# Passes ordered by the weight's part, and 512-column passes in the memory heads' pairs too

## The reference, cut to what matters

```python
h = rms_norm(x, g_pre)                                # x: 512 tokens x 2048
proj = einsum('bsd,de->bse', h, w_in)                 # fp32, all heads' q, k, v and gates
out_a = moba_attention(...)                           # 6 heads, block-sparse causal
out_b = forgetting_attention(...)                     # 6 heads, with a cumulated forget gate
out_m = memory_attention(qm, km, vm)                  # 4 heads into 256 memory tokens
y = concat([out_a * silu(ga), out_b * silu(gb), out_m * silu(gm)])
x = x + rms_norm(einsum('bse,ed->bsd', y, w_out), g_post)
```

## Time and profile before

| | |
|---|---|
| median of 3 runs | 901.62 us (901.34 to 902.13) |
| the profiled execution | 902.28 us, span 900.5 us |
| granted TensorE clock | 0.993 |
| PE busy | 871.3 us, 97% of the span |
| PEld busy | 764.1 us, 85% |
| DVE busy | 733.1 us, 81% |
| ACT busy | 537.8 us, 60% |
| POOL busy | 76.6 us, 9% |
| a weight piece of 512 KB (`raw<-in_w_in`), from issue to landing | 5.4 us, median of 112 |

### The profile page before, as it was taken

The page is one execution under the profiler, slowest core; times in us unless marked ns, Lnnn a source line. Parts: engine busy times, 40 slices in busy tenths (PEclk is TensorE's granted clock), DMA queues, the critical chain, the costliest instruction groups (busy, mean ns, idle before and its releaser), DMA issues.

```text
span 900.5 us, 13815 instructions
## 1 busy us (share of the span) xinstructions
PE 871.3 (97%) x5181; PEld 764.1 (85%) x5181; DVE 733.1 (81%) x1070; ACT 537.8 (60%) x932; POOL 76.6 (9%) x84
## 2 busy tenths in 40 slices
PE   8998999999999999999999999999999999999995
PEld 6888998987888888888888888888888877778884
DVE  5889978888888888888888888888988885975558
ACT  5794665555656565656565656565656585565452
POOL 0000220000000000000030303030301000000000
PEclk9999999999999999999999999999999999999998
DMA  9961567467668568667667667567653397465854
GB/s 304 284 167 48 164 165 154 118 174 164 165 142 210 151 167 185 154 175 177 152 176 175 153 175 175 152 176 175 152 129 106 130 364 272 154 220 189 290 199 186
DMA packets 179143, 161.37 MB, mean 179 GB/s; under 512 B 7353, under 2 KB 144217, under 8 KB 177670
## 3 DMA queue, kind: packets, MB, share of 16 engines
q1 hardware_dynamic: 169942, 141.62, 51.2%
q0 software_dynamic: 8704, 16.78, 13.6%
q10 hardware_dynamic: 432, 2.10, 0.7%
HBM read 152.33 MB, written 43.28 MB: 217 GB/s over the span
## 4 chain that ended last, share of the span: by engine, by line
PE 71%; DVE 15%; ACT 8%; issue 5%; POOL 1%; DVEq 0%; ACTq 0%; POOLq 0%
PE d_ps L703 18%; PE e_ps L703 10%; PE d_ps L705 9%; PE e_ps L705 5%; PE c_ps L703 4%; DVE ring L1459 3%; PE pt_ps L810 3%; ACT ring L1017 3%; PE c_ps L705 2%; PE d_ps L653 2%; PE d_ps L655 2%; PE d_ps L654 2%; DVE sums L1486 2%; PE score_ps L654 1%; PE score_ps L655 1%
## 5 line engine op out<-in xcount | busy, mean ns | idle before, releaser
L1459 DVE TENSOR_TENSOR ring<-raw,ring 128x1024 fp32r<-128x1024 f32 x134 | 164.7, 1231 | 53.1 <-ACT ring L1017 53.0
L703 PE MATMUL d_ps<-late,ring 128*128 128x512 f32 x576 | 206.6, 398 | 1.2 <-DVE five L1586 1.2
L1459 DVE TENSOR_TENSOR ring<-sums,ring 128x1024 fp32r<-128x1024 f32 x112 | 137.6, 1228 | 52.2 <-ACT ring L1017 51.9
L1017 ACT ACTIVATE ring<-raw 128x1024 fp32r<-128x1024 f32 x134 | 140.6, 1058 | 43.8 <-PE d_ps L655 17.2
L705 PE MATMUL d_ps<-late,ring 128*128 128x256 f32 x576 | 161.5, 280 | 0.0
L703 PEld LDWEIGHTS d_ps<-late,ring 128*128 128x128 f32 x576 | 108.1, 188 | 26.4 <-DVE five L1586 1.5
L1017 ACT ACTIVATE ring<-sums 128x1024 fp32r<-128x1024 f32 x112 | 118.1, 1055 | 20.0 <-DVE sums L1486 18.4
L705 PEld LDWEIGHTS d_ps<-late,ring 128*128 128x128 f32 x576 | 108.8, 189 | 0.0
L703 PE MATMUL c_ps<-tok,ring 128*128 128x512 f32 x192 | 69.3, 400 | 0.0
L703 PE MATMUL e_ps<-late,ring 128*128 128x512 f32 x192 | 69.1, 399 | 0.0
L703 PE MATMUL e_ps<-tok,ring 128*128 128x512 f32 x192 | 69.0, 399 | 0.0
(11 more groups left out here) (392 smaller groups left out, 2001.5 us busy)
## 6 DMA issues: line engine op xcount, KB each, us to landing
raw<-in_w_in_dram SPq DMA_DIRECT2D x112, 512.0 KB, 5.4
sum_dram<-in_w_out_dram POOLq DMA_DIRECT2D x32, 512.0 KB, 7.4
raw<-sum_dram SPq DMA_DIRECT2D x32, 512.0 KB, 3.9
raw<-in_w_out_dram SPq DMA_DIRECT2D x24, 512.0 KB, 7.3
raw<-in_w_mem_kv_dram SPq DMA_DIRECT2D x16, 512.0 KB, 8.6
sum_dram<-in_w_out_dram SPq DMA_DIRECT2D x16, 512.0 KB, 6.4
sum_dram<-sum_dram SPq DMA_DIRECT2D x16, 512.0 KB, 6.0
stage<-in_x_dram SPq DMA_DIRECT2D x4, 1024.0 KB, 9.7
```

Source lines behind the costliest of these rows:

```text
L703: pe.matmul(bank[:], w[:, 0, k], both[:, k], start=i in (TOK_A, TOK_B) and k == 0, stop=False, skip_group_check=True)
L1017: act.activation(dst, src, ACTF.Copy).then_inc(hi_done, 1)
L1459: return dve.tensor_tensor(dst, a_, hi_.bitcast(F32), ALU.subtract)
```

## The change

All 28 pairs take the packed form, and within a product the passes are ordered by the weight's part: first the eight passes of 512 columns with the high weights, behind a wait on `hi_done`, and then the eight of 256 columns with the low weights, behind the wait on `lo_done`.

```diff
-        def packed(p):
-            return p >= NM
-
         def merge_count(p, i):
-            return 3 * (p - NM) + [TOK_D, TOK_F, TOK_G].index(i) + 1
+            return 3 * p + [TOK_D, TOK_F, TOK_G].index(i) + 1
...
+                w = weights(operand(p, i))
+                both = both_parts(i)
+                hi = both[:, :, 0]
+                pe.wait_ge(hi_done, operand(p, i) + 1)
+                for k in range(KH):
+                    pe.matmul(bank[:], w[:, 0, k], both[:, k], start=i in (TOK_A, TOK_B) and k == 0, stop=False,
+                              skip_group_check=True)
                 pe.wait_ge(lo_done, operand(p, i) + 1)
-                w = weights(operand(p, i))
-                hi, lo = token_operand(i)
-                both = both_parts(i)
                 for k in range(KH):
-                    if packed(p):
-                        pe.matmul(bank[:], w[:, 0, k], both[:, k], start=i in (TOK_A, TOK_B) and k == 0, stop=False,
-                                  skip_group_check=True)
-                        last = pe.matmul(bank[:, T2:S], w[:, 1, k], hi[:, k], start=False, stop=k == KH - 1,
-                                         skip_group_check=True)
-                        continue
-                    last = three(bank[:, 0:T2], (w[:, 0, k], w[:, 1, k]), (hi[:, k], lo[:, k]),
-                                 i in (TOK_A, TOK_B) and k == 0, k == KH - 1)
+                    last = pe.matmul(bank[:, T2:S], w[:, 1, k], hi[:, k], start=False, stop=k == KH - 1,
+                                     skip_group_check=True)
                 last.then_inc(used, 1)
```

With `packed` gone, its branches are taken by pairs 0 to 3 too: the copies at L1113, L1117 and L1123 and the operations at L1578 and L1582 become 512 columns wide there, `low_half`, `merge` and the halves' sum at L1586 run there, and the high part of q waits for the merge:

```diff
-                if i in (TOK_D, TOK_F, TOK_G) and packed(p):
+                if i in (TOK_D, TOK_F, TOK_G):
                     low_half(p, i)
...
-                if packed(p):
-                    act.wait_ge(merged, merge_count(p, i))
-                else:
-                    act.wait_ge(used, operand(p, i) + 1)
+                act.wait_ge(merged, merge_count(p, i))
...
-                if i in (TOK_D, TOK_F, TOK_G) and packed(p):
+                if i in (TOK_D, TOK_F, TOK_G):
                     merge(p, i)
```

More of the change, by code:

```diff
@@ L1107, in take_product @@
                     act.wait_ge(used, operand(p, i) + 1)
-                cols = slice(0, S if packed(p) else T2)
-                parts = slice(0, 2 if packed(p) else 1)
                 if i == TOK_A:
@@ L1112, in take_product @@
                         first_taken(act, p - 1, 0)
-                    act.activation(c_ps[:, cols], d_ps[p % 2][:, cols], ACTF.Copy, scale=-1.0).then_inc(c_seeded, 1)
+                    act.activation(c_ps[:], d_ps[p % 2][:], ACTF.Copy, scale=-1.0).then_inc(c_seeded, 1)
                 if i == TOK_B:
@@ L1116, in take_product @@
                         late_half_taken(p - 1)
-                    act.activation(five[:, parts], halves(e_ps)[:, parts], ACTF.Copy, scale=-1.0).then_inc(five_taken, 1)
+                    act.activation(five[:], halves(e_ps), ACTF.Copy, scale=-1.0).then_inc(five_taken, 1)
                 if i == TOK_C:
-                    if p > NM:
+                    if p > 0:
                         act.wait_ge(merged, merge_count(p - 1, TOK_G))
-                    elif p > 0:
-                        act.wait_ge(e_less_six, p)
-                    act.activation(one_six[:, parts], halves(d_ps[p % 2])[:, parts], ACTF.Copy).then_inc(six_taken, 1)
+                    act.activation(one_six[:], halves(d_ps[p % 2]), ACTF.Copy).then_inc(six_taken, 1)
             def late_half_taken(p):
@@ L1164, in second_strip @@
                 else:
[L1165 to L1168, removed]
+                    act.wait_ge(merged, merge_count(p, TOK_G))
                     src = d_ps[p % 2][:, 0:T2]
@@ L1577, in take_product @@
                     dve.wait_ge(five_taken, p + 1)
-                    dve.tensor_tensor(halves(e_ps)[:, parts], halves(e_ps)[:, parts], one_six[:, parts], ALU.subtract
+                    dve.tensor_tensor(halves(e_ps), halves(e_ps), one_six[:], ALU.subtract
                                       ).then_inc(e_less_six, 1)
@@ L1581, in take_product @@
                     dve.wait_ge(used, operand(p, i) + 1)
[L1582 to L1587, removed]
+                    dve.tensor_tensor(five[:], halves(d_ps[p % 2]), five[:], ALU.add).then_inc(five_added, 1)
+                    dve.wait_ge(five_added, p + 1)
+                    dve.tensor_tensor(five[:, 0], five[:, 0], five[:, 1], ALU.add).then_inc(last_two_ready, 1)
             def merge(p, i):
@@ L1594, in merge @@
                 dst = high
-                if i != TOK_G and (p - NM) % 2:
+                if i != TOK_G and p >= NM and (p - NM) % 2:
                     half = int(i == TOK_F)
```

## The result

The changed kernel takes 910.74 us (median of 910.80, 910.69, 908.50, 910.78) beside 901.48 us for the kernel before on the same chip: 9.3 us slower. The measured ratio is 1.0089, with a 95% interval of 1.0076 to 1.0101. The profiled execution took 910.8 us with a span of 909.0 (before: 902.28 and 900.5), so 8.5 us of span are to be explained.

What follows compares the result with a forecast made beforehand. PE was taken to bound pairs 5 to 27, the VectorE and ScalarE chain the memory heads' pairs. Terms -4.8 + 0 + 0 + 10.5 = +5.7 us on 901.6 gave 907.3 us, with 899.8 to 912.5 for 8 in 10.

Steps and rivals of the forecast that it cites:

- What bounds the memory heads' pairs: Pairs 1 to 4: PE waits for a serial chain through VectorE and ScalarE; pairs 2 to 4 lose 2 to 3.6 us each.
- part 4: Packed form in pairs 0 to 3 on VectorE and ScalarE: added chain steps start pair 5 10.5 us later, range 8 to 11.5.
- The forget gates' first step: In pair 0, at 106.70 before: 2.8 us later through the packed form's added steps.
- part 3: Packed form in pairs 0 to 3 on PE: 0.107 us less a product, 3.0 us in all, hidden, so taken as 0.
- part 2: The wait on `hi_done`: eight passes run while VectorE makes the low part; gain taken as 0, ends 0 and 1.3 us.
- part 1: Order of passes, pairs 5 to 27: grouping saves 0.44 us a head, 4.8 us over 11 heads, ends 0 and 7.3.
- the unmixed prices: A grouped product of eight wide and eight narrow passes costs what unmixed streams cost, 1.813 + 0.960 = 2.773 us.
- the likeliest case: Whole kernel: a loss of 8 to 11.5 us less a gain of 3.6 to 5.4, so 904.2 to 909.5; chance 0.58.
- the pairs stay PE's: Rival: added steps in the memory heads' pairs run beside PE's high-part passes, no delay handed on; 893.8 us, chance 0.15.
- half of it is covered: Rival: VectorE's gap while ScalarE normalises takes up half the lengthened chain; +5.2 - 4.8, 902.0 us, chance 0.12.
- The order buys nothing: Rival: grouping passes gains nothing, since price may hang on what precedes; +10.5, 912.1 us, chance 0.15.

Runs made afterwards that it cites:

- extra_early: The changed kernel plus four VectorE operations that nothing reads, ahead of the subtraction at L1562 in each of pairs 1, 2 and 3: 913.10 us, ratio 1.0126.
- extra_scalar: The changed kernel plus three ScalarE copies that nothing reads, ahead of D's `low_half` in each of pairs 1 to 3: 912.27 us, ratio 1.0112.
- d_later: The changed kernel with D's `low_half` behind G's high part, and D's merge and part of q behind E's work, in pairs 0 to 3: 909.26 us.
- packed_all_alternating: The changed kernel, packed in all pairs, but with passes alternating and the single wait on the low part as before: 912.05 us, ratio 1.0112.
- pair0_three: The changed kernel with pair 0 alone back in three passes of 256 columns: 907.76 us, ratio 1.0063.
- wait_both: The changed kernel, still grouped, but PE waits for the low part before the 512-column passes: 910.63 us, ratio 1.0095.
- order_three: The kernel of order_only with the 256-column passes of pairs 0 to 3 also grouped, waiting for the parts one by one: 899.88 us, ratio 0.9974.
- order_only: The changed kernel with pairs 0 to 3 back in three passes of 256 columns, passes grouped in pairs 4 to 27 alone: 899.22 us, ratio 0.9969.
- order_fours: The kernel of order_only with each packed product in two groups of four passes of each kind: 901.13 us, ratio 0.999.

## Why the prediction was right, and which term was not

**What bounds the memory heads' pairs: right.** VectorE's busy time grew by 9.95 of the 10.45 us, and extra_early and extra_scalar show by themselves that a step added in the chain is handed on in full, on either engine. That a step taken out gives its time back is not shown: in d_later it did in pair 0 only.

**The packed form, part 4: right in sum, less so in its parts.** packed_all_alternating shows that the form alone costs it. I predicted 10.5 us; measured are 10.45 from the landmark. By pair the forecasts were 4.7, 7.2, 9.8 and 10.5, and the starts came 3.8, 7.0, 10.2 and 10.6 later. The forget gates' first step came at 109.42 instead of 106.70, 2.7 us against 2.8; yet pair0_three shows that only 2.0 of them reach pair 5. From the landmark, pairs 0 and 1 cost 3.64 us together instead of 4.7, pairs 2 and 3 cost 3.25 and 3.19 instead of 2.56 each, and pair 4 cost 0.37 instead of 0.7. My count of added instructions comes to 9.0 of VectorE's 9.95 us. Another 1.3 are in rows that ran longer beside GpSimd (below), less small changes the other way. That the sum is so close is partly luck: these errors have opposite signs.

**PE's own gain there, part 3: right as far as is seen.** Nothing of its 3.0 us shows in the lengths of the pairs; no run isolated it.

**The wait on `hi_done`, part 2: right.** wait_both puts it at 0, order_three too. But its upper end, 1.3 us, rests on a misreading of the earlier trace rows: of the three waits for `ring` only the one of 0.89 us, at 147.51, lies in the pairs. The two others, 0.23 us at 21.41 and 0.22 at 731.05, lie ahead of them and in the output projection, which the change leaves alone.

**The order, part 1: the mis-sized term.** The mechanism holds: order_only is faster, order_fours gives part of it up, and a price by the columns alone, as the prediction takes it from the Trainium skill ("TensorE: Matmul & The Clock Gate", section "Back-to-back issue gap"), does not agree with these runs. The section calls that formula the gap of an isolated matmul, and too high for a stream of 512 columns. Here it is too low for the fp32r passes, 227 ns against its 216, and it fits bf16 passes of the same width, ahead of the pairs: 9.13 - 7.40 = 1.73 us for eight (the rows between are of the same kind).

```profile
7.40 0.59 PE L830 MATMUL pt_ps<-waste 128*128 128x512 bf16 x2
...
9.13 0.59 PE L830 MATMUL pt_ps<-waste 128*128 128x512 bf16 x2
```

What was mis-sized is the step "I take the unmixed prices, 2.773 us". Right behind a narrow stream the wide passes take 1.84 us for eight, so a product costs 2.79: one that had been at 2.83 gains 0.04 and not 0.055, and one that had been at 2.77 loses 0.02. By my count of eight and four a head that is 8 x 0.04 - 4 x 0.02 = 0.24 us; the heads show 0.18, and not the 0.44 of the prediction: 1.95 us instead of 4.8. Matched one by one over the eleven heads, of the 76 products without a wait that stand right behind another product, 48 fall from 2.82 or 2.83 to 2.79 and 28 rise from 2.77 to it, 0.10 us a head together; the 67 behind an attention step give 0.08. The unmixed price was read from streams without a turn, and the earlier trace rows; a grouped product has two turns.

**The sum.** 10.5 - 4.8 = 5.7 became 10.45 - 1.95 = 8.5 us of span. The remaining difference to 9.3 between the medians is within what single executions differ by ahead of pair 0. The time, 910.74, lies inside the range 899.8 to 912.5 but above the likeliest case's own, 904.2 to 909.5. The order's term does that: without its 2.85 us it would be 907.9. Of the rivals, "the pairs stay PE's" and "half of it is covered" are excluded. "The order buys nothing" comes near in time, 912.1, but falls by order_only: a ratio of 0.9969 with its interval below 1.

**What stays open.** Why d_later's earlier `five` is worth 2.5 us inside a pair and 1.1 at the next `normalise` was read from its waits; no run isolated it. Why an alternating product has two prices is open as well; the same product of a head, A for one, is at 2.77 in some heads and at 2.83 in others.

## What to carry to other kernels

Before packing work for TensorE, ask which engine sets the pace of that stage: here the form that saves PE 0.1 us a product puts 2 to 3 us a pair on the chain of the two others, and belongs only in the stages that PE bounds. Count the added steps by stage, on every engine of the chain; here they were paid in full, while taking one out again mostly renamed the wait. And read the price of a pass in the order in which it will run, turns included.

## What the runs showed of the hardware

**The place of the slow clock moves, at no cost here.** TensorE stood at 1.2 GHz once in this part of either kernel. Before, it was as pair 0 began (85 to 88.7 us, granted clock 0.54 on average); after, it is in pair 3, right behind a wait of 1.9 us for `five`. Busy time by engine in steps of 1 us, kernel after:

```profile
190.00:191.00 1.00, 0.00 (x0) 0.00 (x0) 0.97 (x3) 0.04 (x1) 0.00 (x0) 1.00 0.57 100
191.00:192.00 1.00, 0.86 (x3) 0.67 (x4) 1.00 (x2) 0.00 (x0) 0.00 (x0) 0.70 0.95 284
192.00:193.00 1.00, 1.00 (x4) 0.81 (x3) 1.00 (x2) 0.00 (x0) 0.00 (x0) 0.50 1.11 323
...
195.00:196.00 1.00, 1.00 (x9) 0.96 (x8) 1.00 (x3) 0.48 (x2) 0.00 (x0) 1.00 0.00 0
```

The granted clock is 0.50, and eight wide passes take 194.52 - 191.14 = 3.38 us, where 1.81 is the price. VectorE is busy throughout, and that hides it: in wait_both the clock stays up there, and from the `normalise` of pair 3 to that of pair 4 it takes 27.39 us, against 27.38 here.

**GpSimd beside VectorE.** After the change two low parts in pair 1 ran long, 2.10 and 1.62 us instead of 1.22, and one step of `gate` 0.82 instead of 0.43, together 1.7 us. The timeline of DVE and POOL (GpSimd) there, kernel after:

```profile
110.26 3.16 POOL L1986 TENSOR_SCALAR fbuf<-fbuf 6x512 f32<-6x512 f32 x1 [58.29 <-DVE fbuf L1784]
...
111.89 1.28 DVE L1444 TENSOR_TENSOR ring<-sums,ring 128x1024 fp32r<-128x1024 f32 x1 [0.27 <-ACT ring L1012]
...
113.50 1.28 POOL L1987 TENSOR_TENSOR fbuf<-fbuf 6x512 f32<-6x512 f32 x1
...
113.76 2.10 DVE L1444 TENSOR_TENSOR ring<-sums,ring 128x1024 fp32r<-128x1024 f32 x1
114.76 2.46 POOL L1988 TENSOR_SCALAR fbuf<-fbuf 6x512 f32<-6x512 f32 x1
115.79 0.82 DVE L1607 SCALAR_TENSOR_TENSOR gate<-gate,five 128x256 f32<-128x256 f32 x1
...
117.30 2.15 POOL L1990 TENSOR_SCALAR fbuf<-fbuf 6x512 f32<-6x512 f32 x1
118.00 1.62 DVE L1444 TENSOR_TENSOR ring<-raw,ring 128x1024 fp32r<-128x1024 f32 x1
```

In the kernel before VectorE stood idle for the gates in that stretch, and only one row ran long there, by 0.34 us. The Trainium skill ("SBUF — State Buffer", "Who interferes with whom") says that a VectorE instruction with two inputs in SBUF waits until a GpSimd instruction that began first and reads SBUF is done. The low part of 2.10 us fits: GpSimd's L1987 ends at 114.78, and 1.22 us behind that is 116.0, where the row ends at 115.86. Others don't, though spans on GpSimd are rough: the low part at 111.89 took 1.28 us within L1986, which lasts from 110.26 to 113.42; the step of `gate` ended at 116.61, ahead of the end of L1988 at 117.22; and the last low part ended at 119.62, only 0.17 us behind L1990. So the trace bears the rule out in one row and not in these three. No run here took GpSimd's work away, so the cause is argued, not shown.

**Ahead of the first pair.** The landmark lies between 76.5 and 78.5 us over the profiled executions of these fourteen kernels, without regard to the form. A single span can't tell two kernels apart by less than that here; the distances from it to pair 1 and later agree within 0.1 us between kernels that are alike up to there, while those to pair 0 itself still differ by some 0.4 us (8.54 before, 8.97 in order_only).
